# Constant loads, norms, extra expert rows and the last picks re-ordered in a two-block transformer kernel on one core

## What is computed

```python
cond = jax.nn.silu(c)
mod = (cond @ w_mod[i] + b_mod[i])[:, None, :]
shift, scale, gate = jnp.split(mod, 3, axis=-1)
h = rms_norm(x, norm_pre_g[i]) * (1.0 + scale) + shift

top_s, top_i = lax.top_k(s, 16)
best_s, pos = lax.top_k(cand_s, 16)
a = gelu(einsum('cd,ced->ce', xc, expert_down[ic]))
y = einsum('ce,ced->cd', gates * a, expert_up[ic])
```

## Time and profile before

| what | value |
|---|---|
| median of three runs | 1698.29 us |
| the profiled execution | 1696.64 us |
| its span, first to last instruction | 1694.9 us |
| PE, DVE, ACT, POOL busy | 1350.4, 1038.9, 433.6, 483.5 us |
| DMA | 592.02 MB, mean 349 GB/s |
| mean granted TensorE clock | 0.914 of full |

### The profile page before, as it was taken

How to read it: one execution, slowest core, us unless ns; L and a number is a source line. 1 busy time by engine, 2 the same in 40 slices (tenths; PEclk the granted TensorE clock), 3 DMA queues, 4 the chain that set the end, 5 groups by cost and what they waited for, 6 DMA issues and landing times. The chain is left out here.

```text
span 1694.9 us, 13321 instructions
## 1 busy us (share of the span) xinstructions
PE 1350.4 (80%) x3934; PEld 675.0 (40%) x3934; DVE 1038.9 (61%) x2172; ACT 433.6 (26%) x976; POOL 483.5 (29%) x482
## 2 busy tenths in 40 slices
PE   2799978899998999998978669699588646766665
PEld 1354445454444554444543334455234312222222
DVE  5456544644232213116788986898855877778776
ACT  2122323426324321011333232222011221111111
POOL 1101111110000000003445645455444543454441
PEclk9899989999999999999978889798799878888988
DMA  9979896976757677879989989999999999999996
GB/s 380 395 285 380 334 358 223 377 300 245 249 189 270 249 260 260 309 260 353 412 313 416 414 316 413 402 415 414 413 416 414 342 413 420 421 420 421 420 420 260
DMA packets 108828, 592.02 MB, mean 349 GB/s; under 512 B 12211, under 2 KB 12467, under 8 KB 60501
## 3 DMA queue, kind: packets, MB, share of 16 engines
q0 software_dynamic: 67520, 312.52, 46.2%
q1 hardware_dynamic: 41236, 278.65, 43.0%
HBM read 590.08 MB, written 1.05 MB: 349 GB/s over the span
## 5 line engine op out<-in xcount | busy, mean ns | idle before, releaser
L967 PE MATMUL bank<-ring,hT 128*128 128x512 f32 x1888 | 864.0, 614 | 37.9 <-DVE hT L1848 12.9
L967 PEld LDWEIGHTS bank<-ring,hT 128*128 128x128 f32 x1888 | 365.2, 197 | 479.2 <-issue 458.6
L896 POOL DMA_INDIRECT room<-in_peer_down,idx x92 | 101.6, 1104 | 540.8 <-DVE idx L1772 411.9
L1790 DVE CUSTOM_DVE_ANT_0 room<-room 128x1024 f32<-128x1024 f32 x180 | 218.8, 1221 | 58.3 <-DMA room<-in_pair,idx 41.6
L1195 PE MATMUL bank<-room 128*128 128x512 f32 x284 | 159.6, 710 | 97.8 <-ACT room L1486 95.8
L1805 DVE SCALAR_TENSOR_TENSOR x<-room,pcoef,x 128x1024 f32<-128x1024 f32 x121 | 155.7, 1286 | 27.2 <-DMA room<-in_peer_up,idx 26.5
L896 POOL DMA_INDIRECT room<-in_peer_up,idx x104 | 116.7, 1122 | 87.8 <-DVE pa L1790 40.0
L1195 PEld LDWEIGHTS bank<-room 128*128 128x128 f32 x284 | 61.0, 227 | 195.7 <-issue 101.1
L896 POOL DMA_INDIRECT room<-in_pair,idx x88 | 99.5, 1131 | 114.2 <-PE bank L1195 61.2
L946 PE MATMUL bank<-cst,room 128*128 128x128 f32 x424 | 64.7, 296 | 79.0 <-DVE room L1529 40.5
L870 POOL DMA_DIRECT2D room<-in_wmod x80 | 42.2, 528 | 257.8 <-DVE modr L1552 170.2
(11 more groups left out here) (295 smaller groups left out, 1425.8 us busy)
## 6 DMA issues: line engine op xcount, KB each, us to landing
ring<-in_wpk SPq DMA_DIRECT2D x248, 1024.0 KB, 7.5
room<-in_wmod POOLq DMA_DIRECT2D x80, 512.0 KB, 8.8
room<-in_wmod SPq DMA_DIRECT2D x8, 1024.0 KB, 17.2
room<-in_norm_post_g POOLq DMA_DIRECT2D x4, 512.0 KB, 5.1
rowb<-in_gate_bias SPq DMA_DIRECT2D x4, 512.0 KB, 8.9
room<-in_peer_up,idx POOLq DMA_INDIRECT x104, 13.0
room<-in_peer_down,idx POOLq DMA_INDIRECT x92, 13.8
room<-in_pair,idx POOLq DMA_INDIRECT x88, 14.2
```

The source lines that it names most:

```text
L896: return pool.indirect_dma_start(out=dst, out_offset=None, in_=A[table][0] if table != "pair" else A[table], in_offset=bass.IndirectOffset ...
L967: last = mm(bank[p][:, :], lhs, ring[:, h % 4, k * N:(k + 1) * N], start=(kk == 0), stop=(h == halves[-1] and k == 3))
L1790: v.tensor_tensor_reduce(out=row, in0=row, in1=u_(g // MINE), scale=1.0, scalar=0.0, op0=ALU.mult, op1=ALU.add, accum_out=pa[:, g // TOPK ...
```

## The change

Seven edits are made together.

1. `wlow` and `wa2` are loaded right behind the eight early packets, ahead of the first ring halves; `wlow` has a semaphore of its own, `low_in`, and `low` waits for that alone. `consts_in` counts four loads (64). The two `rowb` loads are asked ahead of block `out0` 0 and not of the third block.
2. Each tile of x is loaded one packet earlier; the step `first` of tile 0 sums six pieces before its norm, that of tile 1 two more before its own.
3. Two semaphores become one (`dve_set`).
4. Behind ten blocks named in `LONG`, `spot(4)` stands for `spot(3)`.
5. The first head of tile 1 is chosen in four steps, with a tick behind each of the first three. The first head of tile 0 is four steps too, with nothing between.
6. Pick 251's row is added by PE and not by DVE.
7. The last rows are added at other ticks: 248 to 251 in tick 271, 252 and 253 in tick 273, 254 in 274, 255 in 275; before these were 272, 273, 274 and 275 for the four pairs. The last two picks have a group each.

```diff
 def on_vector(u):
-    return u < 7 * TOPK or (u % 4 == 3 and u < PICKS - 4) or (u % 2 and u < MINE) \
-        or u >= PICKS - 2 or (u % 2 and PICKS - 8 <= u < PICKS - 4)
+    return u < 7 * TOPK or (u % 4 == 3 and u < PICKS - 8) or (u % 2 and u < MINE) or u >= PICKS - 2 or u == PICKS - 7
...
 def added_at(v):
+    if v >= PICKS - 2:
+        return tick_of(v) + 2
     if v >= PICKS - 8:
-        return tick_of(PICKS - 2) + (v - PICKS + 8) // 2
+        return tick_of(PICKS - 2) - 1 + 2 * ((v - PICKS + 8) // 4)
...
-    + [(PICKS - 4, 2), (PICKS - 2, 2)]
+    + [(PICKS - 4, 2), (PICKS - 2, 1), (PICKS - 1, 1)]
...
+LONG = {("in2", 6), ("in3", 0), ("in3", 1), ("in3", 3), ("in3", 5), ("out3", 1), ("hyb", 1), ("hyb", 3), ("hyb", 12),
+        ("hyb", 13)}
...
             if s == ("score_S", 1, 0):
-                order.append(("choose", PH))
+                for part in range(4):
+                    order.append(("choose", PH, part))
+                    if part < 3 and rows.at < MINE + REST:
+                        rows.tick()
...
-            spot(3)
+            spot(4 if mm[2:] in LONG else 3)
...
-                if 1 <= i <= T:
-                    load(x[:, i - 1, :], A["x"][0, (i - 1) * P:i * P, :], f"x_in{i - 1}")
+                if i < T:
+                    load(x[:, i, :], A["x"][0, i * P:(i + 1) * P, :], f"x_in{i}")
+            load(wlow[:, :, :, :], A["wlow"], "low_in")
+            load(wa2[:, :], A["wa2"][:, 0, :], "wa2_in")
...
                     if step == ("mm", 0, "in0", 2):
-                        load(wlow[:, :, :, :], A["wlow"], "consts_in")
-                        load(wa2[:, :], A["wa2"][:, 0, :], "wa2_in")
                         load(cst[:, CST_FIRST:CST_N], A["cst"][:, CST_FIRST:CST_N], "consts_in")
                         load(gmask[:, :, :], A["gla_mask"], "consts_in")
                         load(wsT, A["wsT"], "consts_in")
                         load(posi[:, :], A["pos"], "consts_in")
+                    if step == ("mm", 0, "out0", 0):
                         load(rowb[:, 0, :], A["sgu_ln_g"].to_broadcast([P, D]), "rowb_in")
                         load(rowb[:, 1, :], A["sgu_ln_b"].to_broadcast([P, D]), "rowb_in")
...
                 elif kind == "low":
                     L = step[2]
-                    pe.wait_ge(S("consts_in"), 80)
+                    pe.wait_ge(S("low_in"), 16)
...
                 elif kind == "first":
-                    for n in range(KC if t == 0 else 0):
+                    for n in ((0, 1, 2, 3, 4, 5), (6, 7))[t]:
                         add_piece(n)
                     normalize(t, 0)
```

More of the change, by code:

```diff
@@ L420, in make_order @@
             if name == "query" and n == 1:
-                order.append(("choose", 0))
+                order += [("choose", 0, part) for part in range(4)]
             if name == "query" and n >= 2:
@@ L1080, in _ @@
                     pe.wait_ge(S(f"ln{t}"), 2)
-                    pe.wait_ge(S("wsT"), 1)
+                    pe.wait_ge(S("dve_set"), 1)
                     for g in range(SG):
@@ L1087, in _ @@
                 elif kind == "forget_sum":
-                    pe.wait_ge(S("consts_in"), 80)
+                    pe.wait_ge(S("consts_in"), 64)
                     for j in range(t + 1):
@@ L1423, in _ @@
                         if n < 4:
-                            act.wait_ge(S("gqk"), 1)
+                            act.wait_ge(S("dve_set"), 2)
                         af(k_T(t, n)[rows, :, :].rearrange("p h n -> p (h n)"), bank[c][rows, :], ACT.Copy,
@@ L1668, in angles @@
             def angles():
-                dve.wait_ge(S("consts_in"), 80)
+                dve.wait_ge(S("consts_in"), 64)
                 link(v.tensor_copy(posf[:, :], posi[:, :]))
@@ L1819, in _ @@
                     L = t
-                    for n in range(KC if L == 0 else 0):
-                        add_piece(KC + n)
+                    for n in range(KC, 2 * KC if L == 0 else KC):
+                        add_piece(n)
                     mod_columns(L)
@@ L1919, in _ @@
                     if t == 0:
-                        dve.wait_ge(S("consts_in"), 80)
-                        dve.wait_ge(S("consts_in"), 80)
+                        dve.wait_ge(S("consts_in"), 64)
+                        dve.wait_ge(S("consts_in"), 64)
                         v.tensor_tensor(wsT, wsT, summ.unsqueeze(1).to_broadcast([P, SG, P]), ALU.mult) \
-                            .then_inc(S("wsT"), 1)
+                            .then_inc(S("dve_set"), 1)
                     dve.wait_ge(S("rowb_in"), 32)
@@ L1967, in _ @@
                     if t == 0:
-                        v.tensor_tensor(gqk[:, :], const("gq"), const("gk"), ALU.mult).then_inc(S("gqk"), 1)
+                        v.tensor_tensor(gqk[:, :], const("gq"), const("gk"), ALU.mult).then_inc(S("dve_set"), 1)
                 elif kind == "quad_T" and t == 0:
@@ L1973, in _ @@
                     if n < 4:
-                        dve.wait_ge(S("gqk"), 1)
+                        dve.wait_ge(S("dve_set"), 2)
                         ins = v.tensor_scalar(dst[0:FW, :], bank[c][0:FW, :], gqk[0:FW, :], None, ALU.mult)
@@ L2065, in _ @@
                 elif kind == "choose":
-                    for part in range(4):
-                        choose(t, part)
+                    choose(t, step[2])
                 elif kind == "tick":
```

## The result

| | before | after |
|---|---|---|
| median | 1697.61 us (4 runs) | 1712.66 us (4 runs, 1706.13 to 1714.06) |
| ratio after / before | | 1.0088, 95% interval 1.0059 to 1.0116 |
| profiled execution, span | 1696.64, 1694.9 us | 1706.13, 1704.3 us |
| DMA moved | 592.02 MB | 592.02 MB |

The change makes the kernel 15 us slower; the forecast was 9.7 us faster. The profiled execution of after is the fastest of its four, so the traces explain 9.4 us of the 15 and the rest lies between executions. Lines of the kernel after are shifted by 10 in the step code (L967 is L977, L1790 is L1800).

The account below looks back on a forecast made before the run. PE was taken to bound the kernel up to about 760 us, DMA from 800 us on. Terms -9.0 - 0.5 - 1.8 + 1.6 = -9.7 us took the median of 1698.3 to 1688.6 us, range 1680.5 to 1694.5.

Parts of the forecast that it names:

- Start: First blocks: low no longer waits for pos, PE's lead is 9.5 us, less 0.5 for POOL's pieces: -9.0 us.
- from there on levels of the attention pace PE: After the fourth block: PE waits for evacuation, not DMA, so rowb asked there has room and costs nothing.
- The lead is lost to DVE's pieces before 120 us: Start: one way the change fails to do what it says, leaving only the small terms, 1697.6 us; shared chance 0.07.
- the last rival: Start: low waits for something else, or DVE's pieces eat the lead; only small terms left, 1697.6 us; chance 0.07.
- Rows: Second tile's rows' stage: ticks asked ahead partly fill a DMA hole, between 0 and -2.5, taken as -0.5 us.
- A tick costs DVE 1.22 us for the dot and 1.29 for the add, 2.5 in all: Rows' stage: price of a tick on DVE, matched by 2.5 us of DMA for its two rows.
- only the tick behind in2 6, at the edge of the first: First long DMA hole: this tick alone adds 2.5 us of transfers, against up to 2.5 us more of DVE.
- Each taken away between hyb 3 and hyb 14 gives 2.5 us back for the same reason: Rows' stage: ticks put in earlier are repaid later at 2.5 us each, five against five.
- the ticks are paid and not given back: hyb 3 to 4 and 12 to 14: DMA falls idle, five ticks cost 12.5 us, 1701 us; chance 0.06.
- Choice: Tile 1's first choice, third hole: ticks between parts let two rows be asked inside the hole, -1.8 us (-1.2 to -2.5).
- End: Last adds: a fourth add on PE ends later than DVE's saving, cost between 0 and +1.8, taken as +1.6 us.
- the tests that I set: Wrong if PE's lead is under 5 us at 120 us, not whole at 760, or later stage length differs over 4 us.

Follow-up runs that it names:

- e12: Kernel before with the start's edits (constants ahead, rowb later, norms among first sums, merged semaphore) and 15 modulation pieces in in0 for 17: 1684.36 us, ratio 0.9924.
- e6: Kernel before with a fourth row (tick) behind block in2 6 alone: 1706.90 us, ratio 1.0066.
- e10: e6 with Exp and Gelu of heads 1 to 5 and the choice parts after heads 2 to 5 one tick later: 1702.78 us, ratio 1.0038.
- e14: Kernel before with the fourth row behind hyb 1, 3, 12 and 13 alone: 1695.78 us, ratio 0.9982.
- e11: e6 with one row less behind in3 0, so all stands as before from in3 1 on: 1699.26 us, ratio 1.0010.
- e4: Kernel before with only pick 251's add moved to PE, the last adds at other ticks and the last two picks in own groups: 1699.18 us, ratio 1.0020.
- e1: Kernel before with the start's edits alone (constants ahead, rowb later, norms among first sums, merged semaphore): 1693.95 us, ratio 0.9978.

## Why the prediction was wrong

- **Start, -9.0 forecast (-4.5 to -11.3), -3.7 measured** (-7.1 to -0.3, so the -9.0 is out and the end at -4.5 is not). The first steps held: `pos` gone, `low` 1.92 us at 46.9, next block 11.5 us earlier. The third block started at 59.58 where I took 58, and ran 8.71 us and not 7.5. The step that failed is "from there on levels of the attention pace PE (they wait for the evacuation of PE's block, not for a DMA)". PE's waits are for DVE indeed, but DVE's own are for pieces: 21.5 us of them between 36 and 120 us, 6.6 in the kernel before, and the levels stand behind. The lead at 120 us is 1.8 us. I had asked what the pieces do to the ring's halves, and not what the pieces do to the engine that sums them. "The lead is lost to DVE's pieces before 120 us" stood in the last rival with 0.07, at 1697.6 us; e5, the change without its rows, took 1698.97. e12 shows the price: 5.3 us at this place, of the 9.2 that two pieces give.
- **Rows, -0.5 forecast (0 to -2.5), +16.3 measured.** This made the sign wrong. The step that failed is the price of a row, "A tick costs DVE 1.22 us for the dot and 1.29 for the add, 2.5 in all": a tick also carries the steps that hang on its number, Exp and Gelu with their tables and four parts of a choice. I had put those at nothing, without a reason. Ahead of `in3` 0 they cost PE 4.0 us and open a hole of 4.1 us of transfer in after; with three rows more, ahead of `hyb` 9, 6.7 us and a hole of 4.6. And "only the tick behind in2 6, at the edge of the first, puts 2.5 us of transfers into it, against up to 2.5 us more of DVE" failed as well: PE, DVE and ACT work in turn on one chain there, the row with its part of the choice lengthens it by 3.2 us, and e6 has lost 0.9 us of transfer more by 888 us, not less. These places make up 8.7 us of the holes of after. The rest of the 16.3 is not located: the other new holes are also found where no row is moved, and e10, with the fixed steps back in their places, is still 6.4 us slower.
- **"Each taken away between hyb 3 and hyb 14 gives 2.5 us back for the same reason"** held in `hyb` (e14), and in part in e11, where 3.4 of the 5.9 us come back. In e6, 4.3 us of transfer are lost by 936 us and 5.0 at the end, though its row is taken away again before `hyb` 14. The rival "the ticks are paid and not given back" had the sign and, with 12.5 us, nearly the size, but the wrong place: it named `hyb` 3 to 4 and 12 to 14.
- **Choice, -1.8 forecast (-1.2 to -2.5), +0.8 measured** with an interval from -3.0 to +4.6. The trace gives 8.0 us lost in the third hole before (6.7 and 1.3) and 6.8 after: -1.2, the lower end. The chip cannot tell it.
- **End, +1.6 forecast (0 to +1.8), +3.4 measured** (+0.5 to +6.1). The trace disagrees with the runs. In after, in order of time:

```profile
1686.00 1.23 DVE L1800 CUSTOM_DVE_ANT_0 room<-room 128x1024 f32<-128x1024 f32 x1 [1.26 <-DMA room<-in_pair,idx]
...
1687.86 1.98 PE L1205 MATMUL bank<-ring,room 128*128 128x512 f32 x4 [1.44 <-ACT room L1496]
1689.68 7.03 PE L1205 MATMUL bank<-room 128*128 128x512 f32 x16
...
1696.75 1.29 DVE L2084 TENSOR_TENSOR x<-x,bank 128x512 f32<-128x512 f32 x2 [1.48 <-PE bank L1205]
```

  From the dot of pick 253, the last that waits for its row, to the closing sum it takes 10.75 us; before, from 1676.68 to 1687.25, 10.57. The fourth add costs PE its 1.6 us (7.03 for 5.40), and the coefficients come no sooner: PE takes them up 1.86 us behind that dot in both, as I had it. But the four matmuls there take 1.98 us for 3.44, at a granted clock of 1.00 for 0.56; PE had been idle for 1.44 us ahead of them, and for 3.05 before. That term was not in the sum. Where the other 3 us of e4 come from is open.
- **The whole**: -9.7 forecast, +15 measured. Of the tests that I set, a stage of the rows equal in length to within 4 us failed, as it is 14.5 us longer; 5 us of lead at 120 us failed, with 1.8. That the lead is 5.1 at 760 us is no merit of the change: in e1, with the same start, block `in2` 2 is 1.1 us late. The range, too, was not the sum of its terms, which give 1682.0 to 1694.4 and not 1680.5 to 1694.5.

## What to carry to other kernels

An engine's queue is a schedule: when work is moved by one place, list what hangs on a counter and so moves with it, and look in front of whose chain it now stands. Here one row more ahead of a chain in which three engines work in turn made the chain longer by the whole of the row, and one row less did not make it shorter; so look for the place where the order has no slack left. And a wait that is taken away brings its successor forward into data that have not landed; the small order of those (here two pieces of 512 KB) can be worth more than the wait. Last, a hole in one profile is the change's only if kernels without the change do not have it.

## What was not expected

- Ln and Exp behind a Gelu load tables four times in one norm, 1.28 us each, with the next instruction right behind each load.
- Two pieces fewer at the start take away waits of DVE and PE at 360 us as well, 4.0 us in each of five kernels.
- A row less at four places costs 12.2 us where a row more at one of them costs 11.2: either way from the order before loses.
- Executions of one kernel on one chip scatter by 1% (1691.96 to 1706.84 us in 29 runs). In the profiled executions of kernels that are alike up to 780 us, the rows' stage begins between 2.8 us earlier and 5.3 later. Part of it is there at the third block (up to 3.0 us), up to 4.1 us come between 215 and 400 us, where pieces are still landing, and the rest at single blocks behind.
